# RWKV's last pair: partial products of the output projection with six rows, given to TensorE in the pair's prelude

## What is computed

```python
proj = rmsnorm(x, norm_mix[0]) @ e_w_in            # 1024 x E_COLS
a_out = mixer_a(proj[..., :A_QKV])                 # attention, 256 columns
b_out = mixer_b(proj[..., A_QKV:])                 # RWKV-7, 12 heads of 64, 768 columns
mix = concat([a_out, b_out], -1) @ e_w_out         # 1024 x 1024
x = x + mix
h = rmsnorm(x, norm_mlp[0])
x = x + square(relu(h @ mlp_up)) @ mlp_down
```

## Time and profile before

| | |
|---|---|
| time, median of 3 runs | 3611.16 us (3608.18 to 3612.0) |
| the profiled execution | 3613.97 us |
| its span, first to last instruction | 3612.0 us |
| TensorE busy | 3382.6 us, 94% of the span |
| VectorE, GpSimd, ScalarE busy | 1818.6, 1034.1, 817.9 us |
| mean granted TensorE clock | 0.969 of full speed |

### The profile page before, as it was taken

How to read it: one execution, slowest core, us unless ns; L and a number is a source line. 1 busy time by engine, 2 the same in 40 slices (tenths; PEclk the granted TensorE clock), 3 DMA queues, 4 the chain that set the end, 5 groups by cost and what they waited for, 6 DMA issues and landing times.

```text
span 3612.0 us, 72764 instructions
## 1 busy us (share of the span) xinstructions
PE 3382.6 (94%) x29278; PEld 3229.1 (89%) x29278; DVE 1818.6 (50%) x2980; ACT 817.9 (23%) x1732; POOL 1034.1 (29%) x462
## 2 busy tenths in 40 slices
PE   4999789999997699999999989999997999999998
PEld 4998778888885589999999989999996999999998
DVE  5111684665665545444444473455446744444446
ACT  3344122333332222111111132111111211111112
POOL 2322121110112125333333323222214433333331
PEclk9999799999998899999999999999998999999999
DMA  4212440010011111111111111111121111111111
GB/s 130 71 66 96 142 149 8 31 34 15 22 33 44 56 34 53 47 46 46 41 46 46 47 42 47 61 48 48 50 74 41 47 48 46 46 46 46 46 46 66
DMA packets 80614, 194.68 MB, mean 54 GB/s; under 512 B 9144, under 2 KB 42596, under 8 KB 80264
## 3 DMA queue, kind: packets, MB, share of 16 engines
q1 hardware_dynamic: 37344, 121.39, 10.6%
q10 hardware_dynamic: 43048, 70.01, 5.7%
HBM read 163.86 MB, written 29.86 MB: 54 GB/s over the span
## 4 chain that ended last, share of the span: by engine, by line
PE 79%; DVE 5%; issue 1%; DMA 1%; ACT 1%; ACTq 0%; POOL 0%; DVEq 0%; POOLq 0%
PE psum L245 21%; PE psum L646 20%; PE psum L668 19%; PE psum L3009 3%; PE psum L2022 2%; PE psum L1816 1%; PE psum L2039 1%; PE psum L1996 1%; PE psum L2076 1%; PE psum L2009 1%; DMA s_cache<-cache_a 1%; PE psum L1938 1%; PE psum L2042 1%; DVE b_YX L2712 0%; PE psum L2102 0%
## 5 line engine op out<-in xcount | busy, mean ns | idle before, releaser
L230 POOL TENSOR_TENSOR w_hi<-w_raw,derived 128x1024 fp32r<-128x1024 f32 x215 | 426.3, 1983 | 2336.1 <-PE psum L245 1374.2
L245 PE MATMUL psum<-act_hi,w_hi 128*128 128x352 f32 x2088 | 702.3, 336 | 50.8 <-DVE act_lo L340 23.6
L245 PE MATMUL psum<-act_hi,w_lo 128*128 128x352 f32 x2088 | 678.2, 325 | 0.0
L245 PE MATMUL psum<-act_lo,w_hi 128*128 128x352 f32 x2088 | 677.6, 325 | 0.0
L232 POOL TENSOR_TENSOR w_lo<-w_raw,w_hi 128x1024 fp32r<-128x1024 f32 x215 | 537.2, 2498 | 16.9
L753 DVE TENSOR_TENSOR x<-x,psum 128x352 f32<-128x352 f32 x768 | 385.3, 520 | 233.2 <-PE psum L668 228.2
L668 PE MATMUL psum<-ff_u_hi,w_hi 128*128 128x352 f32 x1536 | 496.6, 323 | 0.0
L646 PE MATMUL psum<-act_hi,w_hi 128*128 128x352 f32 x1536 | 496.0, 323 | 0.1
L668 PE MATMUL psum<-ff_u_lo,w_hi 128*128 128x352 f32 x1536 | 495.0, 322 | 0.0
L668 PE MATMUL psum<-ff_u_hi,w_lo 128*128 128x352 f32 x1536 | 494.7, 322 | 0.0
L646 PE MATMUL psum<-act_lo,w_hi 128*128 128x352 f32 x1536 | 492.4, 321 | 0.0
(11 more groups left out here) (451 smaller groups left out, 4618.7 us busy)
## 6 DMA issues: line engine op xcount, KB each, us to landing
w_raw<-weights SPq DMA_DIRECT2D x215, 512.0 KB, 3.5
s_cache<-cache_a ACTq DMA_DIRECT2D x32, 512.0 KB, 6.7
kv<-a_qkv ACTq DMA_DIRECT2D x12, 528.0 KB, 2.7
x<-x_in SPq DMA_DIRECT2D x3, 1408.0 KB, 16.6
x<-x_in ACTq DMA_DIRECT2D x8, 528.0 KB, 5.5
y<-end_y SPq DMA_DIRECT2D x12, 352.0 KB, 2.4
c_S_s<-state_c ACTq DMA_DIRECT2D x8, 512.0 KB, 3.2
s_c<-c_S_s ACTq DMA_DIRECT2D x8, 512.0 KB, 2.7
```

Of the source, the lines that this page charges most:

```text
L230: pool.tensor_tensor(hi, raw, self.zeros, ALU.add).then_inc(s.sem, s.step())
L245: last = pe.matmul(out, w[:, k, :], h[:, k, cols], start=(start and k == ks[0] and m == 0), stop=(stop and k == ks[-1] and m == 2))
```

## The change

- The loads of rows 0 to 5 and `unit(5, 2, 2)`, the last projection, move from the end of pair 4 and the start of pair 5 to behind pair 4's first half. GpSimd splits the six rows there, and weight tile 2 right behind them, into slot 2.
- In pair 5's prelude TensorE gets six products: output tiles 1 and 2 (`AHEAD`), three chunks each, rows 0 to 5 only (18 matmuls each), at the places of `unit(6, 0, c)` and `unit(6, 1, c)`. ScalarE copies them from PSUM (`keep`) into the two free buffers `raw[0][0:2]`. `begin(0)` with six rows takes the place of `unit(6, 2, 0)`, `begin(1)` that of `unit(6, 2, 1)`, and `more(0)`, `more(1)`, which add row 6, that of `unit(6, 2, 2)`.
- VectorE adds the two buffers to `x` (`dve_parts`), behind the first half of pair 5. ScalarE waits for that before it loads `x` rows 4 to 6, which share the buffers' memory.
- ScalarE loads row 6 in the prelude, for which it waits until pair 4's output is stored; that wait stands in its queue ahead of the copies of the fifth and sixth product.
- In the output stage, tiles 1 and 2 only want rows 6 and 7 (6 matmuls a product). Weight slots: 0, 1, 2, then 0 and 1 in turn; the waits of GpSimd for free slots change with them, those of the MLP's first tiles too.

```diff
         def unit(i, n, c):
-            if i >= self.PAIRS:
-                if (n, c) in ((2, 1), (2, 2)):
-                    out.begin(pe, c - 1)
+            if i > self.PAIRS:
+                return
+            if i == self.PAIRS:
+                if n < 2:
+                    j = NT * n + c
+                    out.early(pe, j, self.unit_bank(i, n, c), self.unit_before(i, n, c) if j < 2 else f"act.out0.early{j - 2}")
+                elif c < 2:
+                    out.begin(pe, c)
+                else:
+                    out.more(pe, 0)
+                    out.more(pe, 1)
                 return
...
             if i + 1 == self.PAIRS:
                 unit(i + 1, 2, 1)
+            if i + 2 == self.PAIRS:
+                unit(i + 1, 2, 2)
             self.pe_near(pe, i, 1)
...
             self.pe_solve(pe, i, 1)
-            unit(i + 1, 2, 2)
+            if i + 2 != self.PAIRS:
+                unit(i + 1, 2, 2)
...
-            if i == self.PAIRS - 1:
-                act.wait_ge(K.sem("s_mix_stored"), 16)
-                act.wait_ge(K.sem("b_out_stored"), (i - 1) * 16)
-                for k in range(KC - 2):
-                    out.load(act, k)
...
-                for k in range(5):
+                for k in range(4):
                     load_x(k)
+                act.wait_ge(K.sem("b_out_stored"), i * 16)
+                out.load(act, KC - 2)
             evacuate(i + 1, 1, 1)
             evacuate(i + 1, 1, 2)
...
             self.act_solve(act, i, 0)
+            if i == self.PAIRS - 2:
+                evacuate(i + 1, 2, 2)
+                act.wait_ge(K.sem("s_mix_stored"), 16)
+                act.wait_ge(K.sem("b_out_stored"), i * 16)
+                for k in range(out.ROWS):
+                    out.load(act, k)
             if i == self.PAIRS - 1:
-                act.wait_ge(K.sem("b_out_stored"), i * 16)
-                out.load(act, KC - 2)
-                load_x(5)
-                load_x(6)
+                for k in out.AHEAD:
+                    act.wait_ge(*at(f"dve.out0.part{k}"))
+                for k in range(4, 7):
+                    load_x(k)
...
             if i == 0:
                 dve.wait_ge(K.sem("s_mix_stored"), 16)
+            if i == self.PAIRS - 1:
+                out.dve_parts(dve, [t[:, 0:T] for t in self.raw[(i + 1) % 2][0:2]])
             self.dve_near(dve, i, 1)
...
+class EarlyProject(Project):
+    ROWS, AHEAD = KC - 2, (1, 2)
+    def slot(self, k):
+        return k if k < 3 else (k - 3) % 2
+    def early(self, pe, j, bank, label):
+        k, c = self.part(j)
+        if j == 0:
+            pe.wait_ge(K.sem(f"{n}_split"), 2 * self.ROWS)
+        if c == 0:
+            K.weight_ready(pe, self.w0 + k)
+        pe.wait_ge(*at(label))
+        K.product(pe, self.slot(k), bank, c, (self.hi, self.lo), range(self.ROWS)).then_inc(s.sem, s.step(f"pe.{n}.early{j}"))
+    def keep(self, act, j, bank, dst, free):
+        act.wait_ge(*at(f"pe.{n}.early{j}"))
+        if c == 0:
+            act.wait_ge(*at(free))
+        act.activation(dst[:, c * TC:(c + 1) * TC], K.psum[:, bank, 0:TC], ACT.Copy).then_inc(s.sem, s.step(f"act.{n}.early{j}"))
+    def dve_parts(self, dve, parts):
+        dve.wait_ge(K.sem("x_loaded"), 16 * 4)
+        for k, part in zip(self.AHEAD, parts):
+            dve.wait_ge(*at(f"act.{n}.early{NT * len(self.AHEAD) - 1}"))
+            dve.tensor_tensor(K.x[:, k], K.x[:, k], part, ALU.add).then_inc(s.sem, s.step(f"dve.{n}.part{k}"))
+    def more(self, pe, m):
+        pe.wait_ge(K.sem(f"{n}_split"), 2 * (KC - 1))
+        K.product(pe, self.slot(0), self.banks[m][0], m, (self.hi, self.lo), range(self.ROWS, KC - 1), start=False, stop=False)
+    def complete(self, pe, m):
+        ahead = k in self.AHEAD
...
+        K.product(pe, self.slot(k), self.banks[m % len(self.banks)][0], c, (self.hi, self.lo),
+                  range(self.ROWS if ahead else KC - 1, KC), start=ahead).then_inc(s.sem, s.step(f"pe.{n}.out{k}.{c}"))
+    def pool(self, pool, before):
+        for k in range(KC):
+            pool.wait_ge(*K.plan.at(before[k] if k < 3 else f"pe.{n}.out{(0, 1, 3, 4, 5)[k - 3]}.{NT - 1}"))
+            K.split_weight(pool, self.w0 + k, self.slot(k))
+            if k == 1:
+                for j in range(self.ROWS):
+                    row(j)
+            if k == 2:
+                row(KC - 2)
```

More of the change, by code:

```diff
@@ L1791, in tail_banks @@
         mean = [(B.of(f"{i}.mean{c}"), f"dve.B.{i}.mean{c}") for c in range(NT)]
-        return [(0, f"act.B.{i}.in2.1"), (1, f"act.B.{i}.in2.2")] + mean + \
+        return [(0, "act.out0.early4"), (1, "act.out0.early5")] + mean + \
             [(B.of(f"{i}.var{c}"), f"act.B.{i}.ln{c}") for c in range(NT)]
@@ L2262, in evacuate @@
         def evacuate(i, n, c):
-            self.evacuate(act, i, n, c)
+            if i < self.PAIRS:
+                self.evacuate(act, i, n, c)
+            elif i == self.PAIRS and n < 2:
+                out.keep(act, NT * n + c, self.unit_bank(i, n, c), self.raw[i % 2][n],
+                         f"pe.B.{i - 2}.RB1e1" if n == 0 else f"dve.B.{i - 2}.lnb")
         for i in range(self.PAIRS + 1):
@@ L2385, in act @@
             self.act_solve(act, i, 1)
-            evacuate(i + 1, 2, 2)
+            if i != self.PAIRS - 2:
+                evacuate(i + 1, 2, 2)
             self.act_y(act, i, 1)
@@ L2480, in act_y, with dve @@
             .then_inc(s.sem, s.step(f"act.B.{i}.y{G}"))
-    def dve(self, dve):
+    def dve(self, dve, out):
         K, plan, ps = self.K, self.K.plan, self.K.psum
@@ L3429, in pool, with part, begin, row @@
                     pool.tensor_tensor(self.lo[:, j], raw, self.hi[:, j].bitcast(F32), ALU.subtract).then_inc(split, 1)
+class EarlyProject(Project):
+    ROWS, AHEAD = KC - 2, (1, 2)
+    def slot(self, k):
+        return k if k < 3 else (k - 3) % 2
+    def part(self, j):
+        return 1 + j // NT, j % NT
+    def early(self, pe, j, bank, label):
+        K, n, at = self.K, self.n, self.K.plan.at
+        s = K.plan.steps["pe"]
+        k, c = self.part(j)
[6 more added lines that the diff above has]
+    def keep(self, act, j, bank, dst, free):
+        K, n, at = self.K, self.n, self.K.plan.at
+        s = K.plan.steps["act"]
+        c = self.part(j)[1]
+        act.wait_ge(*at(f"pe.{n}.early{j}"))
[3 more added lines that the diff above has]
+    def dve_parts(self, dve, parts):
+        K, n, at = self.K, self.n, self.K.plan.at
+        s = K.plan.steps["dve"]
+        dve.wait_ge(K.sem("x_loaded"), 16 * 4)
+        for k, part in zip(self.AHEAD, parts):
+            dve.wait_ge(*at(f"act.{n}.early{NT * len(self.AHEAD) - 1}"))
+            dve.tensor_tensor(K.x[:, k], K.x[:, k], part, ALU.add).then_inc(s.sem, s.step(f"dve.{n}.part{k}"))
+    def begin(self, pe, m):
+        K, n, at = self.K, self.n, self.K.plan.at
+        k, c = divmod(m, NT)
+        rows = range(KC - 1)
+        if m < 2:
+            rows = range(self.ROWS)
+        elif m == 2:
+            pe.wait_ge(K.sem(f"{n}_split"), 2 * (KC - 1))
+        if k in self.AHEAD:
+            return
+        if c == 0:
+            K.weight_ready(pe, self.w0 + k)
+        bank, label = self.banks[m % len(self.banks)]
+        if m >= len(self.banks):
+            kk, cc = divmod(m - len(self.banks), NT)
+            label = f"dve.{n}.add{kk}.{cc}"
+        pe.wait_ge(*at(label))
+        K.product(pe, self.slot(k), bank, c, (self.hi, self.lo), rows, stop=False)
+    def more(self, pe, m):
+        K, n = self.K, self.n
+        pe.wait_ge(K.sem(f"{n}_split"), 2 * (KC - 1))
+        K.product(pe, self.slot(0), self.banks[m][0], m, (self.hi, self.lo), range(self.ROWS, KC - 1), start=False, stop=False)
+    def complete(self, pe, m):
+        K, n, at = self.K, self.n, self.K.plan.at
+        s = K.plan.steps["pe"]
+        k, c = divmod(m, NT)
+        if k == 0:
+            pe.wait_ge(*at(f"dve.{n}.lo{c}"))
+        ahead = k in self.AHEAD
+        if ahead:
+            label = self.banks[m % len(self.banks)][1]
+            if m >= len(self.banks):
+                kk, cc = divmod(m - len(self.banks), NT)
+                label = f"dve.{n}.add{kk}.{cc}"
+            pe.wait_ge(*at(label))
+        K.product(pe, self.slot(k), self.banks[m % len(self.banks)][0], c, (self.hi, self.lo),
+                  range(self.ROWS if ahead else KC - 1, KC), start=ahead).then_inc(s.sem, s.step(f"pe.{n}.out{k}.{c}"))
+    def pool(self, pool, before):
+        K, n = self.K, self.n
+        split, zeros = K.sem(f"{n}_split"), K.derived[:, 1:2].broadcast_to([P, T])
+        def row(j):
+            raw = self.raw[:, j]
+            pool.wait_ge(K.sem(f"{n}_h{j}"), 16)
+            pool.tensor_tensor(self.hi[:, j], raw, zeros, ALU.add).then_inc(split, 1)
+            pool.wait_ge(split, 2 * j + 1)
+            pool.tensor_tensor(self.lo[:, j], raw, self.hi[:, j].bitcast(F32), ALU.subtract).then_inc(split, 1)
+        for k in range(KC):
[6 more added lines that the diff above has]
```

(9 more changed lines are left out.)

## The result

| | before | changed |
|---|---|---|
| median of 4 runs each, us | 3610.3 (3608.18 to 3612.0) | 3565.91 (3565.04 to 3567.54) |
| profiled execution, time and span, us | 3613.97, 3612.0 | 3566.21, 3564.3 |

The ratio is 0.9866, 95% interval 0.9853 to 0.988: 44.4 us less by the medians, 47.7 by the two profiled spans. Forecast were 3561, in a range of 3550 to 3577, and a sum of -50.6.

The account below looks back on a forecast made before the run. TensorE was taken as the bound, busy 94% of the span, with 45.6 us idle in pair 5's prelude and behind its first half. Terms summed to -50.6 us, giving 3560.6 against the median 3611.16; forecast 3561, range 3550 to 3577.

Parts of the forecast that it names:

- What bounds the prelude: Pair 5's prelude: VectorE, held by GpSimd's splits; its row of operations takes 30.5 us there, 11.6 in pair 4.
- The prelude term: Pair 5's prelude, its start included: 60.9 us becomes 35.6, -25.3.
- Early products hide in it: Pair 5's prelude: TensorE's 33 us, new products included, fit barely into the some 35.6 us left.
- The wait behind the first half: Pair 5, behind its first half: `begin(1)` takes 2.9 us in place of 13.2, -10.3; VectorE's two additions cost nothing.
- Pair 4's second half: Pair 4's second half: net +0.5 us for the product moved in, +4.3 for VectorE operations blocked by splits.
- moving the product: Pair 4's second half: `unit(5, 2, 2)` adds 3.8 us in front, saves 3.3 behind the second `pe_solve`, net +0.5.
- the blocking: Pair 4's second half: VectorE's SBUF operations wait for GpSimd's splits, +4.3 us taken between 0 and +8.2.
- blocking in full: Rival, pair 4's second half: all masked copies stand too, up to +26 us over the term, say 3580; chance 0.09.
- Pair 5's second half: Pair 5's second half: `more` has 6 matmuls, 1.0 us in place of 3.5; with ScalarE's last copy, -2.6.
- Output stage: Output stage: 6 products lose 18 matmuls each, -17.2 us; tile 3's weight split is in time by 1.3.
- The sum: Whole kernel: 0.5 + 4.3 - 25.3 - 10.3 - 2.6 - 17.2 = -50.6 us.

Follow-up runs that it names:

- e1: On the kernel before, only the loads of rows 0 to 5, with their GpSimd splits, move into pair 4's second half: 3599.22 us, ratio 0.9944.
- e7: e1 with GpSimd's splits held until ScalarE's last y copy of pair 4, so they still stand in pair 5's prelude: ratio 0.9995.
- e0: The changed kernel run again, unaltered: 3567.33 us, ratio 0.9871 to the kernel before.
- e3: The changed kernel without early products, tiles 1 and 2 multiplied whole in the output stage: 3585.06 us, ratio 0.9901.
- e2: On the kernel before, only row 6's load moves, from behind solve 0 of pair 5 to that pair's prelude: ratio 0.9951.
- e4: The changed kernel with the loads of rows 0 to 5 issued some 10 us later in pair 4's second half: 3559.44 us, ratio 0.9844.
- e6: The changed kernel with both edits, e4's later loads and e5's moved products: 3557.92 us, ratio 0.9841.
- e9: e6 once more, for a second trace and comparison: 3562.57 us, ratio 0.9844.
- e8: e5 with loads left early but GpSimd's splits held until TensorE has done pair 4's sample y: 3563.61 us, ratio 0.9854.
- e5: The changed kernel with row 6's two short products for tile 0 moved to the middle of pair 5's second half: 3565.17 us, ratio 0.9871.

## Why the prediction was right, step by step

The mechanisms of the large terms were right, and experiments show them. The closeness of the term of pair 4's second half is in part luck.

*What bounds the prelude.* Right, and shown: VectorE, held by the splits (e1 against e7, 18.0 us). In the changed kernel the row from copy L2677 (1151.59) to maximum L2560 (1163.23) takes 11.6 us, as forecast. The prelude term was forecast at -25.3 and came to -24.9 (-24.6 in e0).

*Early products hide in it.* Right by e3: taking them out makes the prelude no shorter. `begin(0)` waited as forecast, for ScalarE's copy behind the store wait, idle 3.10 us in front:

```profile
1173.82 0.47 ACT L3485 ACTIVATE b_raw<-psum 128x352 f32<-128x352 f32 x1 [3.10 <-DMA mix<-b_raw]
```

*The wait behind the first half.* -10.3 forecast, -10.1 measured, -9.6 alone in e2. The two additions took 2.42 us beside the 3.06 of `begin(1)`, and VectorE then still waited 0.62 us for TensorE: hidden, as forecast.

```profile
1209.43 2.42 DVE L3494 TENSOR_TENSOR x<-x,b_raw 128x1056 f32<-128x1056 f32 x2
...
1213.08 0.77 DVE L2704 COPY_PREDICATED b_L<-masks,psum 128x256 f32<-128x256 uint8 x2 [0.62 <-PE psum L1964]
```

*Pair 4's second half.* +4.8 forecast, +4.4 measured, +3.1 in e0. It came this near because the kernel before had a clock drop here too: against e2, which has the same program up to there and no drop, the changed kernel's half is 57.8 - 50.2 = 7.6 longer. The parts: with the clock at 1.00, moving the product costs 51.4 - 50.2 = 1.2 (e4 against e2; 0.5 forecast, and e4 still has splits in the half); the blocking costs 3.1 (e1 against e7, a drop in both) where the prediction worked out +2.9 for a drop that recurs and +5.6 for none, and took 4.3 between 0 and 8.2. TensorE's pause behind early loads (2.02 us) it didn't have; in the changed kernel this lies beside VectorE's long products, which are the path. The rule of the Trainium skill (SBUF — State Buffer, Who interferes with whom) that VectorE with two SBUF inputs and GpSimd's reads exclude each other for a whole instruction was seen before at 128 partitions; it now holds at 32 (0.68 becomes 1.53 to 2.80), and its other half, that an operation with at most one SBUF input stays free outside the two-port modes, holds for masked copies (1.33 to 1.38 for two). By the rule alone the blocking was +5.6. The masked copies took the rival *blocking in full* away. One SBUF input isn't enough to be free, though: the 128x8 copy of the earlier trace rows has one, took 1.49 us in place of 0.17 and ended with the split; no run tells in which mode it ran.

*Pair 5's second half.* The one term that missed in the profile of the changed kernel: -2.6 forecast, +0.95 measured. The step (6 matmuls in place of 24, and 0.7 us for ScalarE's last copy) was right: -2.3 in e0, and 46.8 us in e4, 2.2 below the kernel before. What it left out is that TensorE's clock may fall in any second half: it did in that one execution (0.55 over 7.5 us), and it had not in the kernel before's.

*Output stage.* -17.2 forecast; E went from 96.7 to 79.8, -16.9. Tile 3's weights were split from 1279.69 to 1284.08, in time; tiles 1 and 2 had their additions 0.95 us apart.

```profile
1280.99 0.52 DVE L3392 TENSOR_TENSOR x<-x,psum 128x352 f32<-128x352 f32 x1 [0.81 <-PE psum L245]
1281.94 0.52 DVE L3392 TENSOR_TENSOR x<-x,psum 128x352 f32<-128x352 f32 x1 [0.43 <-PE psum L245]
```

*The sum.* By stretches: 4.4 - 24.9 - 10.1 + 0.95 - 16.9 = -46.5; code in front of pair 4's second half that the change doesn't touch gave -1.8 and the rest of the program +0.7, together with rounding -47.7. Forecast was -50.6; the 2.9 between them are less than the 3.55 by which pair 5's second half missed. The medians differ by 44.4 in the first comparison and by 48.8 in e0's, so the forecast was some 2 to 6 us too good. The method has this gap: it takes the clock of one profiled execution for the kernel's. The one of the kernel before had a drop in A and none in D, and e2 and e0 show that either can be otherwise.

*Better than the change.* The loads as in e4 are worth 0.2 to 0.3% more: e4, e6 and e9 at 0.9844, 0.9841 and 0.9844 against 0.9866 and 0.9871, with medians on one chip of 3559.44 and 3557.92 against 3567.33. e4 is the version to keep; whether the later loads or the later splits give it isn't separated (e8), and of e5's part nothing could be measured.

## What to carry to other kernels

When VectorE runs through a row of operations with both inputs in SBUF, look at what GpSimd does beside it, and move that to a place where VectorE reads PSUM: here the same splits of six rows cost 18 us in one place, 3 in another, and at most 1.2 in a third, some ten microseconds further on, where the loads stood later too. To see which, compare the same source lines in two iterations of the loop, one with and one without the neighbour. A term of two or three microseconds in small matmuls should be checked in a second trace, since the clock can take or give as much in code that nobody changed.

## What the runs showed that was not expected

TensorE's granted clock falls to 0.50 for 3 to 10 us in the halves of a pair, at places that differ from one execution to the next. The kernel before and e2 have the same program up to pair 5; their second half of pair 4 took 53.4 us at 0.94 and 50.2 at 1.00. In front of such a drop TensorE had small matmuls and short gaps, but the same work at other times passed without one. The drop of the kernel before cost some 3.2 us here. The time of that kernel over nine runs on one chip, 3610 to 3623 us, would be a few such drops apart, and its two slowest runs have the lowest mean clocks (0.968 and 0.967), its two fastest the highest (0.973); that drops make the scatter isn't shown. Windows of the kernel before, 12.5 us into the half, and of e2 at the same place:

```profile
1102.20:1104.70 2.50, 2.50 (x70) 1.18 (x61) 2.47 (x5) 0.00 (x0) 0.00 (x0) 0.66 0.00 0
1104.70:1107.20 2.50, 2.50 (x22) 2.21 (x23) 0.69 (x2) 0.00 (x0) 0.00 (x0) 0.50 0.03 7
```

```profile
1099.00:1101.50 2.50, 2.50 (x81) 1.69 (x74) 2.47 (x6) 0.00 (x0) 0.00 (x0) 1.00 0.02 7
1101.50:1104.00 2.50, 2.50 (x64) 2.33 (x62) 0.57 (x1) 0.43 (x2) 0.00 (x0) 1.00 0.00 0
```
